# Forgetting attention on one Trainium2 core: the per-head gate rows and the output parts move to other slots, both in one PSUM bank, and the transposes of the probabilities take three banks in turn

## The reference, cut to what matters

```python
def forgetting_attention(q, k, v, log_f):
    F = jnp.transpose(jnp.cumsum(log_f, axis=1), (0, 2, 1))
    def chunk(c):                                   # 4 chunks of 128 positions
        ...
        s = jnp.einsum('bthd,bshd->bhts', qc, k).astype(jnp.float32)
        s = s + Fc[..., :, None] - F[..., None, :]
        p = masked_softmax(s, tpos[:, None] >= kpos[None, :])
        return jnp.einsum('bhts,bshd->bthd', p.astype(v.dtype), v)
```

## Time and profile before

| | |
|---|---|
| median of 3 runs | 1001.13 us (1000.83 to 1001.33) |
| the profiled execution, its own time | 1001.37 us |
| its span, first to last instruction | 999.5 us |
| PE, DVE, ACT, POOL busy | 977.0, 568.5, 410.9, 141.4 us |
| granted TensorE clock | 1.000 in all of the span |
| slots of FOX on PE | from about 478 to 567 us |

### The profile page before, as it was taken

One profiled execution on the slowest core, in us unless ns is written; L12 is line 12 of the kernel. 1 busy time (PEld: TensorE's weight loads), 2 busy tenths in 40 slices (PEclk: granted clock), 3 DMA queues, 4 the chain that ended last, 5 costly groups with the idle time before them and its releaser, 6 DMA issues.

```text
span 999.5 us, 12861 instructions
## 1 busy us (share of the span) xinstructions
PE 977.0 (98%) x4869; PEld 812.6 (81%) x4869; DVE 568.5 (57%) x1162; ACT 410.9 (41%) x752; POOL 141.4 (14%) x185
## 2 busy tenths in 40 slices
PE   6999999999999999999999999999999999999998
PEld 5778788998888888888777788888888888888887
DVE  5747888863565885646555553575556556522113
ACT  5346555544246554445666433432232232221110
POOL 3000000010002112222434230022111112100000
PEclk9999999999999999999999999999999999999999
DMA  6512110103222211322101234222232223223222
GB/s 232 213 48 79 44 43 2 43 5 114 94 84 85 84 45 62 108 85 85 52 35 42 85 120 161 77 108 84 85 119 92 85 96 115 84 88 124 85 85 85
DMA packets 13693, 86.38 MB, mean 86 GB/s; under 512 B 1472, under 2 KB 1984, under 8 KB 4288
## 3 DMA queue, kind: packets, MB, share of 16 engines
q1 hardware_dynamic: 13632, 85.55, 23.7%
HBM read 83.44 MB, written 2.10 MB: 86 GB/s over the span
## 4 chain that ended last, share of the span: by engine, by line
PE 85%; DVE 8%; ACT 4%; issue 3%; DMA 1%; SPq 0%; DVEq 0%; ACTq 0%
PE ps L1429 22%; PE ps L1431 22%; PE ps L1430 22%; PE ps L1614 7%; PE ps L1457 3%; PE ps L1585 3%; DVE wl L938 2%; DVE prob L1148 1%; PE ps L1569 1%; PE ps L1570 1%; ACT prob_f L804 1%; DVE prob_f L1148 1%; PE ps L1484 1%; DVE pt_l L1170 1%; DMA x<-x 1%
## 5 line engine op out<-in xcount | busy, mean ns | idle before, releaser
L938 DVE TENSOR_TENSOR wl<-raw,wh 128x512 fp32r<-128x512 f32 (+2 forms) x118 | 172.0, 1462 | 130.6 <-ACT wh L644 129.0
L644 ACT ACTIVATE wh<-raw 128x2048 fp32r<-128x2048 f32 (+1 forms) x58 | 109.4, 1886 | 151.0 <-PE ps L1431 132.0
L1429 PE MATMUL ps<-aT_h,wh 128*128 128x512 f32 (+1 forms) x376 | 146.7, 390 | 0.9 <-DVE aT_l L947 0.9
L1430 PE MATMUL ps<-aT_l,wh 128*128 128x512 f32 (+1 forms) x376 | 146.4, 389 | 0.0
L1431 PE MATMUL ps<-aT_h,wl 128*128 128x512 f32 (+1 forms) x376 | 146.3, 389 | 0.0
L1429 PE MATMUL ps<-wh,aT_h 128*128 128x512 f32 x256 | 102.2, 399 | 0.0
L1431 PE MATMUL ps<-wh,aT_l 128*128 128x512 f32 x256 | 100.1, 391 | 0.0
L1430 PE MATMUL ps<-wl,aT_h 128*128 128x512 f32 x256 | 99.8, 390 | 0.0
L1429 PEld LDWEIGHTS ps<-aT_h,wh 128*128 128x128 f32 (+1 forms) x376 | 70.0, 186 | 16.6 <-issue 1.1
L1431 PEld LDWEIGHTS ps<-aT_h,wl 128*128 128x128 f32 (+1 forms) x376 | 70.0, 186 | 15.2
L1430 PEld LDWEIGHTS ps<-aT_l,wh 128*128 128x128 f32 (+1 forms) x376 | 70.0, 186 | 15.1
(11 more groups left out here) (234 smaller groups left out, 1774.2 us busy)
## 6 DMA issues: line engine op xcount, KB each, us to landing
raw<-wblk SPq DMA_DIRECT2D x72, 1024.0 KB, 4.8
x<-x SPq DMA_DIRECT2D x4, 512.0 KB, 5.5
w_sb<-w SPq DMA_DIRECT2D x1, 2048.0 KB, 9.2
hid<-x SPq DMA_DIRECT2D x1, 2048.0 KB, 9.0
out<-outt SPq DMA_DIRECT2D x8, 256.0 KB, 2.1
stage<-consts SPq DMA_DIRECT2D x1, 708.5 KB, 4.7
later<-consts SPq DMA_DIRECT2D x1, 448.0 KB, 5.4
par<-params SPq DMA_DIRECT2D x1, 204.5 KB, 8.6
```

Of the source, the lines that this page charges most:

```text
L644: nc.scalar.activation(wh[b % 2][:, 0:n], raw[b % RING][:, 0:n], ACT.Copy).then_inc(hi_ready, 4)
L938: ins = nc.vector.tensor_tensor(wl[b % RING][:, cols], raw[b % RING][:, cols], wh[b % 2][:, cols].bitcast(f32), ALU.subtract)
L1429: nc.tensor.matmul(dst, a_h, b_h, start=start, stop=False)
L1430: nc.tensor.matmul(dst, a_h, b_l, start=False, stop=False)
```

## The change

The change edits the slots of two events and the banks of three. `FB` h moves from slot 4h - 2 to slot 4h - 5 (head 1: from slot 2 to slot 0); `OS` moves one slot later. `FB` (but for head 0's) and `OH` of all heads take bank 2, and the transposes of probabilities take banks 3, 4 and 5 in turn. DVE's wait before it overwrites `osum` is now for `oT_lo` in place of `oT_hi`.

```diff
@@ attention_events
         if h:
-            put(TT * h - 2, "FB", h)
+            put(max(0, TT * h - 5), "FB", h)
         last = TT * h + TT - 1
         put(last + o_lag, "VH", h)
         put(last + o_lag + 1, "OH", h)
         if h % 2:
-            put(last + o_lag + 2, "OS", h // 2)
+            put(last + o_lag + 3, "OS", h // 2)
@@ build
+    def plan_f(key):
+
+        nonlocal turn
+        plan(key, 3 + turn % 3)
         turn += 1
...
             elif e[0] == "A":
-                plan_t(("A", m, e[1]))
+                (plan_f if m == FOX else plan_t)(("A", m, e[1]))
...
             elif e[0] == "FB":
-                plan(("FB", e[1]), 2 + e[1] % 2)
+                plan(("FB", e[1]), 2)
             elif e[0] == "VH":
-                plan(("OH", e[1]), 2 + e[1] % 2)
+                plan(("OH", e[1]), 2)
@@ block.vector
                         if j >= 2 and j % 2 == 0:
-                            dve.wait_ge(oT_hi, TT * FOX + j // 2)
+                            dve.wait_ge(oT_lo, j // 2)
```

More of the change, by code:

```diff
@@ L215, in plan_t @@
         plan(key, 4 + turn % 2)
+        turn += 1
+    def plan_f(key):
+        nonlocal turn
+        plan(key, 3 + turn % 3)
         turn += 1
```

## The result

The changed kernel takes **1009.67 us** (median of 4 runs, 1008.87 to 1010.05), the kernel before 1001.10 us (4 runs, 1000.83 to 1001.33): ratio 1.0085, 95% interval 1.0067 to 1.0102. It is slower, as forecast, but by 8.6 us and not by 4.1, and it lies above the range.

What follows compares the result with a forecast made beforehand. The prediction took the ring of DVE and ACT, not PE, to bound the FOX slots; its slot-by-slot terms summed to +4.1 us, 1005.2 us against the median of 1001.13, in a range of 1001.5 to 1006.9.

Steps and rivals of the forecast that it cites:

- the ring of DVE and ACT: FOX slots: scores on DVE, exponential and `pt_h` on ACT, `pt_l` on DVE, next scores; its length sets the time.
- rival A: FOX slots: PE is the bound and its waits of 2.5 and 2.0 us vanish, 996.6 us; chance 0.10.
- the terms of +1.86 and +2.1: After the fourth exponential: `fb` copy, `VH`, `pt_h` take 2.25 us for 0.39, +1.86; with `OS`, +2.08 or +2.16.
- The copy to `fb`, `OS` and what is hidden: Leaving old slots: `fb` copy -0.48, `OS` -0.65; hidden behind `VH`: `W` piece 0.52 (slot 11), gate copy 0.48 (slot 20).
- C: `W` piece and gate copy add up with `VH`, +1.0, and `VH` halves overlap less, another 0.7: 1006.9 us; chance 0.10.
- B: `VH` doesn't wait for the `fb` copy, so each 1.86 is only 0.48: +1.0, 1002.1 us; chance 0.13.
- the +1.86 of `VH` 0: Slots 7 and 8: PE waits at `VH` for ACT's `fb` copy in bank 2, +1.86 us.
- the +2.08 of slot 15 and `VH` 2: Slots 14 to 16: `fb` copy and `OS` both behind the fourth exponential, 2.47 us where 0.39 passed, +2.08.
- The last row, slot 33, -0.48: Behind the last `VH` that waits: three banks end a transpose's wait for `pt_l`, 0.71 us where 0.23 is usual, -0.48.
- nothing for `OS` behind S31: The table's rows after slot 30 give `OS` no cost; slot 33 holds only the transposes' -0.48.
- The expectations for the profile: Five `VH` waits for `fb`, 1 to 3 us; `pt_l` waits gone; S7 to S9 4.6 us; FOX some 93 us.

Runs made afterwards that it cites:

- e8: Kernel before, with `pt_h` right behind the exponential on ACT and, on DVE, `osum` one slot and `oT_l` two slots later: 990.85 us, ratio 0.9897.
- e5: Changed kernel with transposes in banks 4 and 5, plus 36 unread matmuls into idle bank 3 ahead of `VH` 0 to 4: 1007.1 us, ratio 1.0055.
- e7: Kernel before with `FB` three slots sooner and nothing else: 1001.52 us, ratio 1.0000 to the kernel before.
- e1: Changed kernel once more, no edit, for a second profile: 1009.0 us, ratio 1.0068 to the kernel before.
- e2: Changed kernel's slots for `FB` and `OS`, with the banks of the kernel before: 1004.14 us, ratio 1.0024 to the kernel before.
- e3: Kernel before with the changed kernel's banks and its own old slots: 1002.95 us, ratio 1.0012 to the kernel before.
- e9: Changed kernel with DVE's `oT_l` of heads 4 and 5 one slot later, behind the last reciprocal: 1008.82 us, ratio 1.0068 to the kernel before.
- e6: Kernel before with `OS` one slot later and nothing else: 1004.03 us, ratio 1.0024 to the kernel before.
- e4: Changed kernel with transposes back in banks 4 and 5, bank 3 idle in FOX: 1009.43 us, ratio 1.0072 to the kernel before.

## Why the prediction was right in its mechanism and wrong in its size

**The reading, right.** The kernel is bound by the ring of DVE and ACT. `e8` shows it from the other side: reordering ACT and DVE alone, with PE's list untouched, takes 10.9 us off, although PE was shown busy for 93% of the stretch and 98% of the span. The Trainium skill, "Perfetto Trace Analysis", section "Identifying the Most-Contended Engine", says to find the engine with the highest occupancy and to optimize that first, and warns that the busy share of matmuls is no good measure of how close one is to the roofline. The warning holds here: the 82.85 of 89.00 busy us of PE left 6.2 us to win, and `e8` has `VH` 7 10.0 us sooner. These are the same rows with which rival A argued.

**Bank 2, the terms of +1.86 and +2.1: mechanism right, sizes right at full clock.** `e5` has 1.85 for the first. Its parts, at `VH` 1 of the changed kernel, are 0.63 from `fb` (509.11) to `VH` and 1.60 from there to `pt_h`, 2.23 for the 0.73 + 1.52 = 2.25 that I had priced. Each part is off, by 0.10 and by 0.08, in opposite directions; that the sum fits to 0.02 is luck.

**The copy to `fb`, `OS` and what is hidden: right.** `e7` has 0.47 to 0.49 for the copy. The step from S13 to S17, which holds two `OS` terms, is +0.98 in `e5` for +0.95; from S21 to S25 it is +1.04 for +1.03. The `W` piece and the gate copy are hidden: S11 to S13 +1.35 for +1.34, S17 to S21 +0.90 for +0.90. So C, that they add up, is refuted, and so is B for the changed kernel. The time came out above C's bound for reasons that no rival had.

**The step that failed first: the +1.86 of `VH` 0 and the +2.08 of slot 15 and `VH` 2 were priced at full clock.** The prediction made PE wait 1 to 3 us in five places, and costed what follows the wait with rows in which PE had hardly waited. In `VH` 0 and `VH` 2 PE ran at 1.2 GHz: for `VH` 0 it is 0.83 us from `fb` to `VH` and 2.67 from there to `pt_h`, 3.50 in place of 2.25, and 1.15 us from `pt_h` to S9 (500.83 to 501.98) in place of 0.90. That is the +1.49; with +1.12 in slot 16 it makes **2.6 us** (1.95 in `e1`), shown by the clock in both profiles of the changed kernel and by `e5`, which takes it away. The Trainium skill, "Perfetto Trace Analysis", section "Matmul Optimizations", says it in one line: the matmul engine "dynamically scales power based on utilization, so it's important that matmuls execute back-to-back in batches". The trace agrees, with 0.57 where PE had paused for 2.54 and 3.23 us and 1.00 in `e5` where it had not; but a pause alone doesn't settle it, since `e2` shows 1.00 behind 2.44 us. The five waits that the prediction itself announced were the place to apply it.

**The last row, slot 33, -0.48, and nothing for `OS` behind S31: wrong in sign, +0.66 measured.** The miss of 1.14 us has two parts. The transposes' wait for `pt_l` did go, but the bank's gain was over-sized: PE would soon have had to wait for POOL's scaling anyway, and `e3`, the banks alone, gives 0.18 and not 0.48. That is 0.30. The other 0.84 is `OS` in slot 31 (7.36 us from S31 to `VH` 7 in after against 6.52 in `e3`). I had priced it on the ring only, where it costs nothing behind S31. But `oT_l` stands on DVE ahead of the reciprocal that POOL waits for, and PE waits 0.93 us for POOL. `e9`, with the reciprocal first, gets 0.35 of it back; the other 0.5 is POOL's slower pair, shown but not explained. With two banks (`e6`) `OS` costs 0.68 there, with the wait for `pt_l`. So the third bank exchanges one wait for the other: 7.36 us in after, 7.38 in `e4`.

**The start, +0.85**, is not tied to the change by anything here: `e9` and `e1` run the same instructions in the first mixer, and the stretch at half clock came in `e1` and not in `e9`. The first set of runs of before, 1001.10 us, was at the low end of the later ones, 1001.42 to 1001.73; against those of its own chip the changed kernel is +7.6 (`e1`), and its two profiles have `VH` 7 at +7.83 and +7.18: 4.12 forecast, 1.1 behind S31, 2.6 and 1.95 for the clock. What decides whether that stretch comes is open.

**The expectations for the profile** held: five waits of 0.8 to 3.2 us for `fb`, waits for `pt_l` gone, ACT waiting in front of `pt_h`. The distance of S7 to S9 was 6.09 us and not 4.6, and this is where the first error could be seen at once; the FOX slots took some 97 us on PE (89 + 7.8) and not 93.

## What to carry to other kernels

When an engine is near full and short waits move around on it, look whether two other engines release each other in turn; then price a change on that ring, and put every copy that the next turn doesn't need behind the instruction that it does need (`e8`: -10.9 us for an order of lists). Before two results share a bank, ask in whose queue the read of the first stands and what it waits for: the same two results in one bank cost 5.3 us as `VH` behind `fb` (`e4` above `e2`), of which some 3.2 us at full clock (`VH` 7 at +5.23 in `e5`, at +2.08 in `e2`), and 1.5 us as `FB` behind `osum` (`e3`), by the estimate there mostly through the clock. Wherever a forecast makes TensorE wait for some 2 us or more, as it did in slots 8 and 16 here, add a line for the work behind the wait at the lower clock, as a case of its own with a chance of its own.

## What the runs showed of the hardware

- Behind idle times of PE of 1.8 to 3.2 us the granted clock fell to its lower level for a stretch (0.57 over 4 us behind 2.54 and 3.23 us in after, 0.58 behind 2.33 us in `e3`), and didn't fall behind 1.10 us. The length of one idle time doesn't decide it alone: behind 2.37 and 2.44 us in `e2` it stayed 1.00. Of one and the same wait of `VH` 4 for `fb`, it stayed 1.00 behind 1.77 us in after and 1.78 us in `e9`, and fell to 0.66 over 5 us behind 1.81 us in `e1` and 1.78 us in `e4`. What else decides it no run here shows.
- The fall can come within `VH`, or before it: in `e4`, `VH` 0 itself took its usual 0.82 us and the clock was 0.71 over 497 to 502 us, while for `VH` 2 it fell in the idle time.
- Filling the idle time with matmuls that nothing reads kept the clock at 1.00 in all of FOX, and with 8.3 us more of PE's work `e5` stands 2.6 us lower above the kernel before than `e4` (5.4 against 8.0). It is a test, not a remedy; `e8` removes the idle time itself.
- A matmul of 512 columns in the middle of a row of them starts 0.23 us behind the one before at 2.4 GHz and 0.43 us at 1.2 GHz (in `e3`, 544.53 to 544.96).
